# A finer table of TensorE's steps, other places of the steps beside it, and VectorE's weight subtraction cut in two in the last stage

## The chip, the cores and the metric

The program runs on one core of one Trainium2 chip. The metric is the device time of one execution in microseconds (us), as the median of three runs of the same program.

## What is computed

A sequence of 256 tokens of width 1024, in float32, goes through two layers of one kind and then through two of another, and at the end through a norm.

```python
for l in range(2):                                    # first block
    h = h + 0.5 * rms_norm(swiglu(rms_norm(h, g1), w_gate, w_up, w_down), p1)      # 1024 -> 2816 -> 1024
    u = rms_norm(h, mix_pre_g[l])
    (a_b, a_c, a_x, b_u, c_q, c_k, c_v, d_q, d_k, d_v, d_f, gate_logits) = split(u @ w_in[l])
    y_a = (a_b * conv3(a_c * a_x)) @ a_w_out
    y_b = silu(layer_norm(conv31(glu(b_u)) + bias)) @ b_w_out
    y_c = difference_attention(c_q, c_k, c_v) @ c_w_out          # two softmaxes, the second times lambda
    y_d = forgetting_attention(d_q, d_k, d_v, d_f) @ d_w_out
    h = h + rms_norm((sum of sigmoid(gate) * y over the four) @ w_o[l], p2)
    h = h + 0.5 * rms_norm(swiglu(rms_norm(h, g2), ...), p3)
for l in range(2):                                    # second block, "hybrid"
    z = rms_norm(h, norm_g[l]) @ w_in_2[l]
    qa, ka = axial_rope(rms_norm(aq)), axial_rope(rms_norm(ak))  # heads normed and rotated
    oa = attention(qa, ka, va) * silu(ag)
    ob = windowed_attention_with_sink(rope(bq), rope(bk), bv) * silu(bg)
    qc = rms_norm(cq) @ c_wuq ; kv = rms_norm(ckv) @ c_wukv      # the latent branch
    oc = attention([qc_nope, rope(qc_rope)], [kc_nope, rope(ckr)], vc) * silu(cg)
    h = h + concat(oa, ob, oc) @ w_out[l]
out = rms_norm(h, final_g)
```

## The kernel before

Every weight is read once from HBM, in chunks of 128 partitions by up to 2048 columns, in the order in which they are used (LOAD). SyncE issues the loads into `raw`, a ring of five slots; the load of chunk c waits until chunk c - 5 has been used up (semaphore `used`). Precision is kept by splitting each number into a high and a low part: ScalarE rounds a chunk to `whi` (L696), VectorE subtracts it from `raw` and leaves `wlo` in the same slot (L1046, semaphore `lo_v`), and TensorE makes three products for each pair of tiles (`mm3`, L1573 to L1575). Activations are split in the same way (`xhi`, `xlo`). "split n" below is the step that does ScalarE's or VectorE's half of this for the chunk that stands n places after the first of the stage.

The stages follow each other on one stream: twice (feed-forward, "mix", feed-forward), then twice "hybrid". Between two stages stands `boundary`: the result is normed and added to h in two halves of 128 tokens (t = 0, 1), the next norm is made, TensorE turns it (`turns`, L1671), ScalarE copies the turned tile to `xhi` (L715) and VectorE subtracts (`low`, L1065). TensorE meanwhile begins the next stage on t = 0 (`wide_entry`, L1641 to L1647).

Inside mix and hybrid the order of each engine is a list that is made once: `mix_steps` and `hybrid_steps` give every step a number, the place, and sort by it. Whole chunks of weights stand at regular places, and the small steps of the attentions, the convolution and the norms are put between them: `scores` (q times k), `max` and `exp`, `weigh` (VectorE, one over the sum), `turn` (TensorE transposes the probabilities, L1907 in mix, L2056 in hybrid), `copy`, `values` (times v, L1921, L2071, L2079) and `o_copy`, and then `flip` (transposes of q and k, or of the result). Each engine runs its list strictly in order, and each step first waits for the semaphores of its inputs. So a step whose input is late holds up all that stands behind it on its engine. In the hybrid stage TensorE's chunks could be entered by other steps at their middle, between the two halves of tokens; in the mix stage not at all. SyncE's list is the order of the loads alone; GpSimd's holds the powers for the norms (L659), in the order in which they are needed.

The names that matter: `l_norm` (L1477, L1478) norms the latent columns, after `l_square` on ScalarE (L975) and GpSimd's power; `l_turn` (L2014) is TensorE's transpose of them. `ropeg` (L1434) folds gains into the rotation tables for `a_rotate`. `o_split` (L1389) makes the low part of an attention's result, and `turn` 5 of the mix stage waits for it, since both use the same bank.

Of the kernel before, what the change touches and what calls it, by code (L numbers as in the profile page):

```python
# [14 lines left out]
ALU = mybir.AluOpType  # L15
# [6 lines left out]
P = 128  # L22
# [159 lines left out]
def mix_steps():  # L182
# [10 lines left out]
    for slot, (kind, n) in enumerate(chunks):  # L193
        pe.append((slot + 0.5, kind, n))
# [5 lines left out]
    at(pe, (19.02, 21.02, 23.02, 25.04, 27.02, 29.02, 31.02, 33.02), "turn")  # L200
# [22 lines left out]
             16.55, 17.55, 18.55, 19.55, 21.05, 22.05, 23.05, 23.55, 24.55, 25.55, 26.55, 28.057, 28.55, 30.55, 31.0601,  # L223
# [3 lines left out]
    at(dve, (25.5, 28.5, 31.5, 34.5, 37.5, 40.5, 43.5, 46.5), "out")  # L227
# [4 lines left out]
             19.06, 20.06, 21.0447, 22.06, 23.06, 24.06, 24.1, 25.1, 25.5275, 26.08, 28.14, 29.08, 30.12, 31.08, 32.12,  # L232
# [8 lines left out]
    at(dve, (18.02, 20.02, 22.02, 24.02, 26.02, 28.02, 30.02, 32.02), "weigh")  # L241
# [35 lines left out]
def hybrid_steps():  # L277
# [11 lines left out]
    at(pe, (3.52,), "l_turn")  # L289
    at(pe, (6.02, 6.2376, 6.54, 6.56, 9.02, 9.04, 10.52, 10.54), "flip")  # L290
    at(pe, (6.58, 7.54, 9.06, 9.54, 10.04, 10.58, 11.04, 12.04, 12.54, 14.04), "scores")
    at(pe, (7.52, 8.52, 9.5539, 10.02, 10.56, 11.02, 12.02, 12.52, 14.0607, 14.52), "turn")
    at(pe, (7.58, 8.54, 9.9373, 10.08, 10.62, 11.08, 12.08, 12.58, 14.08, 14.54), "values")
    at(act, (0.91, 1.9031, 1.91, 2.91, 4.6801, 5.91, 6.91, 8.91, 9.0669, 9.2882, 10.91, 11.3652, 12.91, 13.91, 14.4), "split", range(3, 18))
    at(act, (1.4, 1.9, 3.9, 4.0105, 4.0985, 4.2, 5.2, 5.7, 7.4, 7.9, 9.4, 9.9), "take", TAKES)
    at(act, (2.54,), "l_square")
    at(act, (3.52,), "l_hi")
    at(act, (6.02, 6.52, 6.54, 6.56, 9.02, 9.04, 10.52, 10.54), "flip_copy")
    at(act, (6.6, 7.56, 9.08, 9.56, 10.06, 10.6, 11.36, 12.06, 12.56, 14.06), "exp")
    at(act, (7.52, 8.52, 9.52, 10.02, 10.56, 11.32, 12.02, 12.52, 14.02, 14.52), "copy")  # L300
# [28 lines left out]
def program(nc, stream, x_in, pre_gain, post_gain, par1, par2, cst_in, out):  # L329
    ctx = ExitStack()  # L330
    with ctx:
# [704 lines left out]
        def _(dve):  # L1036
# [31 lines left out]
            def boundary(X, i, q, ch, share=None, last=False):  # L1068
# [6 lines left out]
                for t in range(NT):  # L1075
                    for n in range(2):
# [11 lines left out]
                        if t and not last:  # L1088
                            low(X + 1, 0, n)
# [1144 lines left out]
```

## Time and profile before

| | |
|---|---|
| median of 3 runs | 1691.02 us (1689.95 to 1692.52) |
| the profiled execution | 1691.12 us |
| its span, from the first to the last instruction | 1689.3 us |
| TensorE (PE) busy | 1646.0 us, 97% of the span |
| VectorE (DVE) busy | 1098.7 us, 65% |
| ScalarE (ACT) busy | 815.8 us, 48% |
| granted TensorE clock | 0.997 of full speed |
| read from HBM | 290.23 MB, 172 GB/s over the span |

The span is 1.8 us shorter than the execution's own time; the rest lies before the first and behind the last instruction. The first block fills the span up to about 1403 us, the two hybrid stages what is left. A row of the timeline gives the start, the duration, the engine, the source line and in brackets how long the engine was idle just before it and what ended the wait.

### The profile page before, as it was taken

The page shows a single profiled execution, that of the slowest core. Times are in us where ns is not written, and L with a number is a line of the kernel's source. Part 1 is how long each engine was busy: PE and PEld are TensorE (multiplying, and loading weights), DVE is VectorE, ACT ScalarE, POOL GpSimd, SP SyncE. Part 2 cuts the span into 40 slices and gives each one's busy share as a digit, 9 for nine tenths or more (in the row PEclk, how much of TensorE's full clock was granted, in tenths as well). Part 3 has the DMA queues.
Part 4 walks back from the last instruction along what each step waited for, and adds up shares of the span by engine and source line. Part 5 has one row for each costly group of instructions (what it writes and reads, how often), then busy time and mean ns, then how long its engine had stood idle before and what let it go on. Part 6 is the DMA issues. An engine that isn't in the chain of part 4 may idle for free.

```text
span 1689.3 us, 21552 instructions
## 1 busy us (share of the span) xinstructions
PE 1646.0 (97%) x8719; PEld 1395.1 (83%) x8719; DVE 1098.7 (65%) x1314; ACT 815.8 (48%) x1116; POOL 36.5 (2%) x60
## 2 busy tenths in 40 slices
PE   8999999999999999999999999999999998999997
PEld 7888799978887888788888998788888887778776
DVE  6444668898666454655456799975665455766665
ACT  5443544454445443454445454544544446664653
POOL 0000000000000000000000000000000000000000
PEclk9999999999999999999999999999999999999999
DMA  8555465444556555565546545355555545224421
GB/s 311 196 179 199 165 219 178 162 175 150 175 174 218 181 195 182 179 216 181 194 155 224 189 168 193 126 174 195 192 206 193 181 150 162 100 93 141 135 75 50
DMA packets 67427, 292.70 MB, mean 173 GB/s; under 512 B 7152, under 2 KB 11648, under 8 KB 51456
## 3 DMA queue, kind: packets, MB, share of 16 engines
q1 hardware_dynamic: 63984, 279.47, 48.2%
q10 hardware_dynamic: 3344, 11.85, 2.0%
q8 instruction: 69, 1.13, 0.3%
q14 instruction: 30, 0.25, 0.0%
HBM read 290.23 MB, written 1.06 MB: 172 GB/s over the span
## 4 chain that ended last, share of the span: by engine, by line
PE 82%; DVE 9%; issue 3%; ACT 3%; DVEq 2%; DMA 1%; POOL 0%; ACTq 0%; POOLq 0%; SPq 0%
PE ps L1573 24%; PE ps L1575 24%; PE ps L1574 24%; DVE wlo L1046 3%; PE ps L2045 2%; PE ps L1736 1%; DVE mix L1243 1%; DVEq L1248 1%; PE ps L2071 1%; PE ps L1671 1%; ACT tmp L699 1%; PE ps L2056 1%; PE ps L1708 1%; PE ps L1641 1%; DVE small L1335 1%
## 5 line engine op out<-in xcount | busy, mean ns | idle before, releaser
L1046 DVE TENSOR_TENSOR wlo<-raw,whi 128x2048 fp32r<-128x2048 f32 (+2 forms) x269 | 601.2, 2243 | 259.4 <-ACT whi L696 253.9
L696 ACT ACTIVATE whi<-raw 128x2048 fp32r<-128x2048 f32 (+2 forms) x269 | 500.3, 1872 | 130.7 <-DMA raw<-stream 129.4
L1573 PE MATMUL ps<-whi,xhi 128*128 128x512 f32 (+1 forms) x1024 | 404.1, 395 | 1.1 <-ACT mix L960 1.1
L1575 PE MATMUL ps<-whi,xlo 128*128 128x512 f32 (+1 forms) x1024 | 396.2, 387 | 0.0
L1574 PE MATMUL ps<-wlo,xhi 128*128 128x512 f32 (+1 forms) x1024 | 396.2, 387 | 0.0
L1573 PE MATMUL ps<-whi,yar 128*128 128x512 f32 x620 | 245.5, 396 | 2.0 <-DVE yar L1560 1.5
L1574 PE MATMUL ps<-wlo,yar 128*128 128x512 f32 x620 | 241.0, 389 | 0.0
L1575 PE MATMUL ps<-whi,yar 128*128 128x512 f32 x620 | 241.0, 389 | 0.0
L1573 PEld LDWEIGHTS ps<-whi,xhi 128*128 128x128 f32 x1024 | 192.8, 188 | 40.7 <-issue 4.5
L1575 PEld LDWEIGHTS ps<-whi,xlo 128*128 128x128 f32 x1024 | 192.7, 188 | 39.0
L1574 PEld LDWEIGHTS ps<-wlo,xhi 128*128 128x128 f32 x1024 | 192.9, 188 | 35.3
L1573 PE MATMUL ps<-xhi,whi 128*128 128x256 f32 (+1 forms) x720 | 207.5, 288 | 0.0
L1574 PE MATMUL ps<-xlo,whi 128*128 128x256 f32 (+1 forms) x720 | 203.6, 283 | 0.0
L1575 PE MATMUL ps<-xhi,wlo 128*128 128x256 f32 (+1 forms) x720 | 203.5, 283 | 0.0
L1573 PEld LDWEIGHTS ps<-whi,yar 128*128 128x128 f32 x620 | 116.4, 188 | 30.8 <-issue 7.2
L1573 PEld LDWEIGHTS ps<-xhi,whi 128*128 128x128 f32 (+1 forms) x720 | 136.3, 189 | 3.3 <-issue 0.9
L1574 PEld LDWEIGHTS ps<-xlo,whi 128*128 128x128 f32 (+1 forms) x720 | 136.4, 189 | 1.9
L1575 PEld LDWEIGHTS ps<-xhi,wlo 128*128 128x128 f32 (+1 forms) x720 | 136.3, 189 | 0.5
L1575 PEld LDWEIGHTS ps<-whi,yar 128*128 128x128 f32 x620 | 116.4, 188 | 24.3
L1574 PEld LDWEIGHTS ps<-wlo,yar 128*128 128x128 f32 x620 | 116.5, 188 | 23.0
L758 ACT ACTIVATE yar<-ps 128x512 fp32r<-128x512 f32 x44 | 26.3, 597 | 177.8 <-PE ps L1736 177.8
L1243 DVE SCALAR_TENSOR_TENSOR mix<-mix,par 128x256 f32<-128x256 f32 x240 | 105.2, 480 | 5.3
(217 smaller groups left out, 1361.6 us busy)
## 6 DMA issues: line engine op xcount, KB each, us to landing
raw<-stream SPq DMA_DIRECT2D x262, 512.0 KB, 4.7
raw<-stream SPq DMA_DIRECT2D x122, 1024.0 KB, 4.8
raw<-stream SPq DMA_DIRECT2D x22, 384.0 KB, 3.9
gpre<-pre_gain ACTq DMA_DIRECT2D x8, 512.0 KB, 4.2
gpost<-post_gain ACTq DMA_DIRECT2D x6, 512.0 KB, 5.3
mix<-cum ACTq DMA_DIRECT2D x2, 1024.0 KB, 6.8
raw<-stream SPq DMA_DIRECT2D x6, 256.0 KB, 6.8
raw<-stream SPq DMA_DIRECT2D x4, 320.0 KB, 4.4
```

Of the source, the lines that this page charges most:

```text
L696: A(whi[:, s, 0:w], raw[:, s, 0:w], ACT.Copy).then_inc(hi_ready, 1)
L699: A(tmp[:, n * 512:(n + 1) * 512], src, ACT.Square, scale=1.0 / 32, accum_out=rq[:, t, col + n:col + n + 1]).then_inc(sq_done, 1)
L758: A(hhi[hbuf(g)].rearrange("p m t -> p (m t)"), bank(2), ACT.Copy).then_inc(hhi_done, 1)
L1046: TT(wlo[:, s, 0:w], raw[:, s, 0:w], whi[:, s, 0:w].bitcast(F32), ALU.subtract).then_inc(lo_v, 1)
L1243: ins = STT(out=acc_b[:, m, :], in0=v, scalar=w, in1=acc_b[:, m, :], op0=ALU.mult, op1=ALU.add)
L1248: dve.drain()
L1335: dve.tensor_reduce(sm[:, 8:12], prob[:, :, 0:nk], AX, ALU.max)
L1573: pe.matmul(dst, lh, rh, start=first, stop=False)
L1574: pe.matmul(dst, lh, rl, start=False, stop=False)
L1575: return pe.matmul(dst, ll, rh, start=False, stop=last)
L1641: pe.matmul(dst, xhi[:, kk, rows_], wide_k(whi, c + j, k), start=(kk == 0), stop=False)
L2045: ins = pe.matmul(sc[:, e, :], a[:, t * P:(t + 1) * P], b, start=True, stop=True)
```

## The change

Five things change.

1. TensorE's list is cut finer. In the hybrid stage a chunk of weights is now eight parts (two halves of tokens, each in four) and an output chunk two; in the mix stage every chunk is two. Only the places between the parts are new: the same matmuls are made, in the same order inside a chunk.
2. The places of nearly all steps of the hybrid stage are new, on TensorE, ScalarE and VectorE; in the mix stage those of `turn` 4 on TensorE and of six steps on VectorE: two taps of the convolution move forward (18 and 19 of the second half of channels), split 26 moves behind `values` 4, `out` 2 behind `values` 6, and two `weigh` get other numbers without passing anything.
3. In the hybrid stage VectorE's split of a chunk is two steps, `half_split` (the first half of the columns) and `split` (the second half), each of half the width; the wait for `whi` is in the first, `lo_v` is raised by the second. In the new table the two stand next to each other for each of the 15 chunks.
4. In `boundary`, where a gain is applied (`share`), VectorE's last subtraction for t = 0 (`low(X + 1, 0, 1)`) moves from ahead of the update of h for t = 1 to behind it.
5. The wait for the rotation tables (`cst_in_s`) moves from `ropeg` to the start of VectorE's hybrid list, and `ropeg` moves behind `ck_rotate`.

SyncE's and GpSimd's lists are what they were, and no DMA changes its place among those of its queue.

```diff
@@ mix_steps (two of the lines of its table)
     for slot, (kind, n) in enumerate(chunks):
-        pe.append((slot + 0.5, kind, n))
+        for half in range(2):
+            pe.append((slot + 0.5 + half / 20, kind, (n, half)))
-    at(pe, (19.02, 21.02, 23.02, 25.04, 27.02, 29.02, 31.02, 33.02), "turn")
+    at(pe, (19.02, 21.02, 23.02, 25.04, 27.1998, 29.02, 31.02, 33.02), "turn")
@@ hybrid_steps (the parts, and one of the lines of its table)
     for p in range(AT_WOUT):
-        for half in range(2):
-            pe.append((p + half / 2 + 0.4, "chunk", p, half))
+        for part in range(8):
+            pe.append((p + (0.4, 0.425, 0.45, 0.475, 0.9, 0.925, 0.95, 0.975)[part], "chunk", p, part // 4, part % 4))
     for n in range(4):
-        pe.append((AT_WOUT + n / 2 + 0.4, "out", n))
+        for part in range(2):
+            pe.append((AT_WOUT + n / 2 + 0.4 + part / 20, "out", n, part))
+    at(dve, (1.9244, 1.9679, 2.4195, 4.1735, ...), "half_split", range(3, 18))
@@ VectorE
-            def split(ch):
+            def split(ch, half=None):
...
-                dve.wait_ge(hi_ready, ch + 1)
                 w = chunk_width(ch)
-                TT(wlo[:, s, 0:w], raw[:, s, 0:w], whi[:, s, 0:w].bitcast(F32), ALU.subtract).then_inc(lo_v, 1)
+                cut = slice(w // 2 if half == 1 else 0, w // 2 if half == 0 else w)
+                if half != 1:
+                    dve.wait_ge(hi_ready, ch + 1)
+                ins = TT(wlo[:, s, cut], raw[:, s, cut], whi[:, s, cut].bitcast(F32), ALU.subtract)
+                if half != 0:
+                    ins.then_inc(lo_v, 1)
@@ boundary
-                        if t and not last:
+                        if t and not last and not (share and n):
                             low(X + 1, 0, n)
                     dve.drain()
                     if share:
...
                                 op0=ALU.mult, op1=ALU.add).then_inc(h_ready, 1)
+                        if t:
+                            low(X + 1, 0, 1)
                         mean_square(q + (4 * t + 4), t, 2)
                         normed(t, i * 2 + (2 * t + 2))
@@ VectorE, hybrid
+                dve.wait_ge(cst_in_s, 32)
                 for step in HYB_DVE:
                     kind, n = step
-                    if kind == "split":
-                        split(ch + n)
+                    if kind == "half_split":
+                        split(ch + n, 0)
+                    elif kind == "split":
+                        split(ch + n, 1)
                     elif kind == "ropeg":
                         dve.wait_ge(par_in, l * 16 + (16 * DEPTH + 16))
-                        dve.wait_ge(cst_in_s, 32)
@@ TensorE: features, wide_tokens and rows_of take the parts (one of the three)
-            def wide_tokens(c, b, t):
+            def wide_tokens(c, b, t, ks=range(4)):
                 half = WIDE[c][2]
-                for k in range(4):
+                for k in ks:
...
+                if 3 not in ks:
+                    return
@@ TensorE, hybrid
-                        _, p, half = step
+                        _, p, half, part = step
...
                         if name in Z_PAIRS:
-                            if i == 0:
+                            if i == 0 and part == 0:
                                 hyb_free(pe, l, p, half)
-                            wide_tokens(c, half, half)
+                            wide_tokens(c, half, half, (part,))
```

What that does to the lists is seen at three places. In the rows an instruction reads: line, operation, out<-in, shape and what it waits for.

The first is TensorE's list in the mix stage, behind the chunk at place 26. `ps<-cst,prob` is `turn` 4, `ps<-mix` is `scores` 5, `ps<-whi,...` are matmuls with weights. Before:

```order
L1575 MATMUL ps<-whi,xlo 128x512
L1907 MATMUL ps<-cst,prob 128x128 [waits o_read,p_ready]
L1907 MATMUL ps<-cst,prob 128x128 x7
L1892 MATMUL ps<-mix 128x256 [waits nm_ready]
L1892 MATMUL ps<-mix 128x256 x3
L1573 MATMUL ps<-whi,xhi 128x512 [waits lo_v]
```

And with the change:

```order
L1586 MATMUL ps<-whi,xlo 128x512
L1911 MATMUL ps<-mix 128x256 [waits nm_ready]
L1911 MATMUL ps<-mix 128x256 x3
L1926 MATMUL ps<-cst,prob 128x128 [waits o_read,p_ready]
L1926 MATMUL ps<-cst,prob 128x128 x7
L1584 MATMUL ps<-whi,xhi 128x512 [waits lo_v]
```

`scores` 5 has passed `turn` 4; on VectorE, between `values` 3 and `scores` 5, a split of 2048 columns (split 26) has gone and stands behind `values` 4.

The second is ScalarE's list at the start of the hybrid stage. `mix<-ps` are the copies of the latent columns, `tmp,rq<-mix` is `l_square`, `yar<-ps` is the copy behind `l_turn`. Before:

```order
L967 ACTIVATE mix<-ps 128x352 [waits wide_done]
L967 ACTIVATE mix<-ps 128x352 [waits used]
L696 ACTIVATE whi<-raw 128x768 [waits landed3]
L696 ACTIVATE whi<-raw 128x512 [waits landed4]
L975 ACTIVATE tmp,rq<-mix 128x192 [waits evac_a]
L977 ACTIVATE tmp,rq<-mix 128x128
L975 ACTIVATE tmp,rq<-mix 128x192 [waits evac_a]
L977 ACTIVATE tmp,rq<-mix 128x128
L696 ACTIVATE whi<-raw 128x2048 [waits landed0]
L996 ACTIVATE yar<-ps 128x256 [waits lat_t]
```

And with the change:

```order
L699 ACTIVATE whi<-raw 128x768 [waits landed3]
L970 ACTIVATE mix<-ps 128x352 [waits wide_done]
L970 ACTIVATE mix<-ps 128x352 [waits used]
L978 ACTIVATE tmp,rq<-mix 128x192 [waits evac_a]
L980 ACTIVATE tmp,rq<-mix 128x128
L978 ACTIVATE tmp,rq<-mix 128x192 [waits evac_a]
L980 ACTIVATE tmp,rq<-mix 128x128
L699 ACTIVATE whi<-raw 128x512 [waits landed4]
L999 ACTIVATE yar<-ps 128x256 [waits lat_t]
```

`l_square` now stands ahead of the split of 512 columns and its wait for a load, and the split of 2048 columns behind the copy. On TensorE `l_turn` has moved one half chunk (12 matmuls) forward.

The third is TensorE's list in the hybrid stage around `turn` 1 (`ps<-cst,gpost`) and `values` 1 (`ps<-probT_b,mix`). Before:

```order
L1575 MATMUL ps<-whi,xlo 128x384
L2056 MATMUL ps<-cst,gpost 128x128 [waits pt_ready,p_ready]
L2056 MATMUL ps<-cst,gpost 128x128 x7
L2079 MATMUL ps<-probT_b,mix 128x128 [waits o_read,evac_a,pt_ready]
L2079 MATMUL ps<-probT_b,mix 128x128 x7
```

And with the change (three quarter chunks, of which the matmuls of two are left out here, and `values` 0 now stand between the two):

```order
L2077 MATMUL ps<-cst,gpost 128x128 [waits pt_ready,p_ready]
L2077 MATMUL ps<-cst,gpost 128x128 x7
L1584 MATMUL ps<-whi,xhi 128x384 [waits evac_a]
L1585 MATMUL ps<-wlo,xhi 128x384
L1586 MATMUL ps<-whi,xlo 128x384
L2100 MATMUL ps<-probT,mix 128x128 [waits evac_a,qkt_a,pt_ready]
L2100 MATMUL ps<-probT,mix 128x128 x7
...
L2100 MATMUL ps<-probT_b,mix 128x128 [waits o_read,evac_a,pt_ready]
L2100 MATMUL ps<-probT_b,mix 128x128 x7
```

What stood directly behind its supplier now has matmuls with weights in between.

## Rows read from the trace of the kernel before

**Rows 1.** The page: busy time by engine

```profile
PE 1646.0 (97%) x8719; PEld 1395.1 (83%) x8719; DVE 1098.7 (65%) x1314; ACT 815.8 (48%) x1116; POOL 36.5 (2%) x60
```

**Rows 2.** Waits of TensorE over the whole span: us in total, times, longest

```profile
PE ps L1671 <- DVE mix L1059: 6.1, 6, 2.4
...
PE ps L1907 <- DVE mix L1365: 4.6, 2, 2.3
PE ps L2056 <- DVE gpost L1543: 3.2, 6, 1.0
PE ps L2045 <- ACT mix L1004: 2.8, 4, 0.7
PE ps L2079 <- ACT probT_b L1025: 2.2, 2, 1.1
PE ps L2014 <- DVE mix L1478: 2.1, 2, 1.2
```

**Rows 3.** Five windows: length, busy PE, PEld, DVE, ACT, POOL; clock, DMA share, GB/s

```profile
1409.30:1530.00 120.70, 110.99 (x634) 92.54 (x633) 81.37 (x139) 72.35 (x151) 5.09 (x6) 1.00 0.32 109
1550.70:1672.00 121.30, 112.25 (x633) 93.69 (x633) 81.04 (x143) 69.45 (x148) 5.08 (x6) 0.99 0.30 103
1455.58:1460.01 4.43, 3.85 (x19) 3.08 (x19) 3.21 (x4) 3.28 (x8) 0.00 (x0) 1.00 0.40 168
1596.93:1602.25 5.32, 5.32 (x18) 4.33 (x18) 3.80 (x5) 3.87 (x8) 0.00 (x0) 0.68 0.36 149
1457.07:1459.43 2.36, 2.36 (x13) 2.04 (x12) 2.17 (x3) 1.21 (x6) 0.00 (x0) 1.00 0.13 49
```

**Rows 4.** Timeline of VectorE at the first boundary

```profile
201.07 0.69 DVE L1083 SCALAR_TENSOR_TENSOR thb<-ps,gpost 128x512 f32<-128x512 f32 x1
201.67 0.68 DVE L1065 TENSOR_TENSOR xlo<-ps,xhi 128x512 fp32r<-128x512 f32 x1
202.46 1.41 DVE L1095 SCALAR_TENSOR_TENSOR h<-thb,rs,h 128x512 f32<-128x512 f32 x2
```

**Rows 5.** Timeline of GpSimd there, then of TensorE

```profile
201.24 0.55 POOL L659 TENSOR_TENSOR rs<-rtmp,halft 128x1 f32<-128x1 f32 x1 [4.55 <-DVE rtmp L1051]
...
203.71 1.98 PE L1647 MATMUL ps<-whi,xlo 128*128 128x512 f32 x8
206.44 1.32 PE L1671 MATMUL ps<-cst,mix 128*128 128x128 f32 x8 [0.75 <-DVE mix L1059]
```

**Rows 6.** Timeline of TensorE in the first mix stage

```profile
366.75 1.07 PE L1907 MATMUL ps<-cst,prob 128*128 128x128 f32 x8 [2.29 <-DVE mix L1365]
367.74 1.14 PE L1892 MATMUL ps<-mix 64*128 64x256 f32 x8
...
382.38 1.03 PE L1907 MATMUL ps<-cst,prob 128*128 128x128 f32 x8
```

**Rows 7.** Timeline of VectorE there

```profile
368.60 2.29 DVE L1046 TENSOR_TENSOR wlo<-raw,whi 128x2048 fp32r<-128x2048 f32 x1
...
381.07 0.68 DVE L1389 TENSOR_TENSOR yar<-ps,yar 128x512 fp32r<-128x512 f32 x1
```

**Rows 8.** Timeline of ScalarE, then of VectorE, at the start of the first hybrid stage

```profile
1409.41 0.46 ACT L967 ACTIVATE mix<-ps 128x352 f32<-128x352 f32 x1 [2.95 <-PE ps L1647]
...
1412.56 0.63 ACT L696 ACTIVATE whi<-raw 128x512 fp32r<-128x512 f32 x1 [1.95 <-DMA raw<-stream]
1413.09 0.35 ACT L975 ACTIVATE tmp<-mix 128x192 f32<-128x192 f32 x1
...
1416.39 0.35 DVE L1478 SCALAR_TENSOR_TENSOR mix<-mix,rs,par 128x128 f32<-128x128 f32 x1
```

**Rows 9.** Groups of VectorE by shape: xcount | busy us, mean ns | idle before

```profile
L1046 DVE TENSOR_TENSOR wlo<-raw,whi 128x2048 fp32r<-128x2048 f32 x253 | 577.8, 2291 | 252.8 <-ACT whi L696 247.5
...
L1231 DVE TENSOR_TENSOR mix<-tmp,mix 128x1024 f32<-128x1024 f32 x12 | 14.7, 1226 | 0.9
```

**Rows 10.** DMA issues: KB each, median us from issue to landing

```profile
raw<-stream SPq DMA_DIRECT2D x122, 1024.0 KB, 4.8
```

More of the change, by code:

```diff
@@ L292, in hybrid_steps @@
[L292 to L298, printed above, removed]
@@ L306, in hybrid_steps @@
-    at(dve, (2.52,), "ropeg")
-    at(dve, (2.54,), "l_norm")
-    at(dve, (3.52,), "l_lo")
-    at(dve, (5.52,), "cq_rotate")
-    at(dve, (5.54,), "ck_rotate")
-    at(dve, (6.58, 7.54, 9.06, 9.54, 10.1064, 10.58, 11.04, 12.04, 12.54, 13.746), "max")
-    at(dve, (6.64, 7.62, 9.1, 9.62, 10.12, 10.66, 11.12, 12.1, 12.62, 14.1), "weigh")
-    at(dve, (8.02,), "a_mean")
-    at(dve, (8.02, 8.03), "a_rotate")
-    at(dve, (10.1, 10.11), "b_rotate")
-    at(dve, (10.9, 11.9, 12.9, 13.9), "gate")
-    at(dve, (11.1, 13.52, 15.02), "o_gate")
@@ L318, in hybrid_steps @@
-    at(dve, (11.7636, 13.53, 15.03), "o_low")
+        for part in range(2):
+            pe.append((AT_WOUT + n / 2 + 0.4 + part / 20, "out", n, part))
+    at(pe, (3.1197,), "l_turn")
+    at(pe, (5.4052, 6.1126, 6.4028, 6.4617, 8.9693, 9.1434, 10.4986, 10.6243), "flip")
+    at(pe, (6.9147, 7.4596, 9.4166, 9.906, 10.1901, 10.62, 10.9953, 11.4463, 11.9932, 12.9718), "scores")
+    at(pe, (8.4312, 8.5133, 9.9185, 10.3524, 10.9726, 11.0352, 12.4819, 12.935, 13.926, 14.0062), "turn")
+    at(pe, (8.9199, 8.966, 10.0387, 10.6179, 11.0096, 11.4335, 13.57, 13.9328, 14.016, 14.4175), "values")
@@ new lines, in hybrid_steps @@
+    at(act, (0, 0, 1.2009, 3.0722, 6.6004, 7.3136, 7.3484, 7.4213, 9.2391, 9.7951, 9.8875, 11.5645, 11.9264, 13.5379, 14.4885), "split", range(3, 18))
+    at(act, (0, 0, 4.8269, 5.2691, 5.8413, 6.4056, 6.4179, 6.4845, 7.4475, 7.5446, 9.2565, 9.5613), "take", TAKES)
+    at(act, (0.0543,), "l_square")
+    at(act, (1.5895,), "l_hi")
+    at(act, (6.4341, 6.5396, 6.7871, 7.1083, 8.5071, 8.847, 10.1345, 10.2488), "flip_copy")
+    at(act, (7.3987, 7.4945, 9.2075, 9.56, 9.721, 10.2087, 11.5264, 11.8831, 13.0461, 13.5386), "exp")
@@ new lines, in hybrid_steps @@
+    at(dve, (1.9245, 1.968, 2.4196, 4.1736, 5.8115, 6.8876, 6.8982, 9.0102, 10.2115, 10.2743, 11.024, 12.0727, 13.5213, 15.1284, 15.3818), "split", range(3, 18))
+    at(dve, (5.7505,), "ropeg")
+    at(dve, (2.2601,), "l_norm")
+    at(dve, (2.3134,), "l_lo")
+    at(dve, (5.57,), "cq_rotate")
+    at(dve, (5.69,), "ck_rotate")
+    at(dve, (6.88, 7.3612, 9.06, 9.54, 10.1035, 10.2663, 10.8198, 11.1546, 12.1934, 12.6207), "max")
+    at(dve, (8.0675, 8.0891, 9.3, 10.103, 10.2354, 10.2817, 11.9676, 12.5579, 12.6742, 13.0818), "weigh")
```

124 lines of the change are left out of this document (67 added, 57 removed).

## The prediction

> **What bounds the kernel now.** I read the page first: TensorE is busy for 1646.0 of 1689.3 us, and VectorE and ScalarE have a third and half of the span free [rows 1]. The amount of matmul work is the same before and after, so the time can only move by what TensorE waits, and all its waits together are the difference, 43 us. Next comes the list of TensorE's waits, which says for whom [rows 2]. Some 5 us lie at the start, where nothing is changed. Three places are left that the change touches: the turn of the second token half at the six boundaries, 6.1 us; one wait in each of the two mix stages for VectorE's L1365, 4.6 us; and a dozen kinds of short waits in the hybrid stages. The windows add those up [rows 3]: in the first stage 120.70 - 110.99 = 9.71 us idle, in the second 121.30 - 112.25 = 9.05. VectorE is busy for 81 of 121 us there and ScalarE for 72: neither is full, so these are waits for latency, where TensorE stands directly behind its supplier. The reader is to see in them that a wait of 0.6 to 1.2 us disappears as soon as that much other TensorE work is put in front of it.
>
> **The boundary.** VectorE reads thb until 201.07 + 0.69 = 201.76, then does the subtraction L1065 that is moved, and begins the update of h at 202.46 [rows 4]. The other thing that the update needs is GpSimd's power, done at 201.24 + 0.55 = 201.79 [rows 5]. Without the subtraction the update can begin at about 201.85, 0.6 us earlier, and squares, power, norm and turns follow it. TensorE waits there for 0.75 us [rows 5], so the gain fits inside. What is late next is the moved subtraction itself: behind the two updates (1.41 us) it ends at 201.85 + 1.41 + 0.6 = 203.9. The matmuls that read it are the second four of L1647's eight, from 203.71 + 1.98/2 = 204.7: 0.8 us of cover. It also sits in time that VectorE spent waiting for ScalarE's squares. At the sixth boundary (into the hybrid stage) the wait is 2.4 us [rows 2], the matmuls are narrower and those four may come late by 0.6, but in front of a longer wait. Six times 0.61: **3.7 us**. Bounds: nothing if the power is late, 6 x 0.7 = 4.2 at most.
>
> **The mix stage.** TensorE stands idle for 2.29 us until 366.75, because `turn` 4 waits for `values` 3 on VectorE, which goes from one instruction straight to the next there and is simply behind. With `scores` 5 first, 1.14 us of work fills the gap [rows 6]; its inputs are long there. The rest of the wait stays, since VectorE's sum of work up to there is the same (the two taps only trade places). What is late next is `turn` 5: it started at 382.38 [rows 6] and would now come at 381.2, but it waits for `o_split` 0, which ended at 381.07 + 0.68 = 381.75 [rows 7]. The 2.29 us split that is taken from 368.60 goes back in before it, so it ends no earlier (0.4 less where a short gap closes). So of 1.14 about 0.65 us stays, twice: **1.3 us**. Bounds 0.6 and 2.5. `out` 2 is put 3 us later, and its reader comes 10 us later; the same move frees `weigh` 7.
>
> **The hybrid stages.** I walked the new order step by step with the durations of the trace. At the start ScalarE copied the latent columns at 1409.41, then waited 1.95 us for a load, and came to the squares at 1413.09; now the squares follow the copy at 1409.8, 3.3 us earlier, so `l_norm` ends at 1413.4 and not at 1416.74 [rows 8]. TensorE arrives at `l_turn` at 1413.3, since it stands one half chunk (2.1 us) earlier: 0.2 us of its 1.2 are left. At `values` 1 (1.1 us) three quarter chunks, 3 x 0.59 from the half chunk of 2.36 [rows 3], and `values` 0 (2 us) stand in front: gone. Walked like this, the waits for L1543 (`weigh`), for the copies, for L1469 and for L1560 all fall under cover; VectorE has `weigh` done 1 to 9 us before TensorE asks. Two do not go. `scores` 2 still waits for the last `flip` copy, about 0.1. `scores` 3 waits for `exp` 2, which can only begin behind `scores` 2 and `max` and is over 4.43 - 1.56 = 2.9 us after `scores` 2 [rows 3], and the cover is four quarters as before: 0.58 stays. First stage: 9.71 - 0.88 = **8.8 us**.
>
> In the second stage the clock comes in. Between `scores` 2 and `scores` 3 the stretch takes 5.32 us where the first stage has 4.43, at a granted clock of 0.68 against 1.00 [rows 3]: for 3.4 us TensorE ran at 1.2 of its 2.4 GHz, after several waits in a row. Those waits are the ones that go. So 9.05 - 0.3 = **8.75**, and 5.32 - 4.43 = **0.9** if the clock holds; nothing of the latter if it falls anyway.
>
> **The cost of the halves.** The halves are neighbours, so nothing can use the point between them. A subtraction of 2048 columns takes 2291 ns, the like of 1024 columns 1226 [rows 9]: 161 ns more for a pair by durations, under 0.1 from start to start, 30 times 0.08 to 0.16 = 2.4 to 4.8 us of VectorE. I cost it at nothing: the cover is VectorE's 40 us of idle time in each stage. At four points (`l_turn`, `turn` 1, `scores` 2, `turn` 2) my walk leaves less than 0.3 us, and I take **1 us** off for these.
> The Trainium skill speaks against this step: "VectorE: DVE Perf Modes", section "The TRN2 errata — SBUF-src ops pay a fixed extra latency per instruction", says that one large tile pays the fixed cost once and many small ones each time, and gives an fp32 tensor_tensor (N + 151)/0.96 ns. By that formula, which the row of 2291 ns agrees with, a pair costs 157 ns more, 4.7 us in all.
>
> The `ropeg` step (1.3 us) moves behind `ck_rotate`; its reader comes some 15 us later. The wait for the tables was met hundreds of us before.
>
> **Sum.** 3.7 + 1.3 + 8.8 + 8.75 + 0.9 - 1 = 22.45, say 22.5 us. The profiled execution took 1691.12 us (span 1689.3), 0.1 above the median of the three runs: 1691.1 - 22.5 = **1668.6 us**, 1.3% faster.
>
> **Rivals.** (a) The walk is right, 0.52: between 1665.5 and 1671.5.
> (b) The waits come back at other places, 0.22. When TensorE is 9 us earlier at the end of a stage, every supplier must be so too, and VectorE and ScalarE have chains of their own (`scores`, `max`, `exp`, `weigh`, `copy`). Against it: they wait for TensorE much of the time. If half of the 17.5 us returns, 1668.6 + 8.8 = 1677.4.
> (c) The halves' cost reaches the path, 0.10: every 161 ns delays TensorE, 30 x 0.161 = 4.8 us: 1673.4. For it speaks that a split now often stands just before `max` or `weigh`; against it that most of those have over 1 us. The skill's rule named above, taken as deciding, would give this too: 1673.3.
> (d) More is gained than the waits show, 0.07: the busy time of pipelined matmuls may hide stalls, and the sixth boundary's low clock may go: 1660 to 1665.
> (e) Slower, 0.05: ScalarE now has splits 8, 9 and 10 ahead of `exp` 0 and `exp` 1, and waits for their loads in front of the softmax. Chunk 9's slot is free at about 1422, and `exp` 0 must be over at 1434.6, with 5 us of ScalarE work between: the load may take 7.5 us, and takes 4.8 [rows 10]. Only if loads there took over 18 us would each stage lose more than the whole change gains, and the time be 1695 or so.
> (f) The change doesn't do what it says, 0.04: the stages and boundaries are tied by chains through all engines, and the waits only change their names: a gain of 1 or 2 us, 1689.5.
>
> **Range and chances.** From the lower part of (a) and some of (d), over (c), to the far side of (b): 1664 to 1680, with 0.8 inside; (a)'s own is 1665.5 to 1671.5. A measurement of this kernel tells 0.2%, 3.4 us, from no change. Faster: (a) to (d), 0.91. Within: most of (f), 0.04. Slower: 0.05.
>
> **What would show it.** The wait of L1671's successor at five boundaries at 0.15 us, at the sixth 1.7; TensorE's wait before `turn` 4 at 1.15, with a new one of about 0.5 before `turn` 5; about 1 us idle in each hybrid stage, 0.58 of it before `scores` 3; no second fall of the clock; a pair of halves about 2.4 us long on VectorE. TensorE busy for 1646 us as before, less what the clock gave. I would be wrong if waits for `exp`, `weigh` or `whi` appear behind `scores` 4, where my walk has cover of several us, or if TensorE's busy time grew with the number of pieces.

## The result, and the profile after

The changed kernel takes 1662.92 us (median of 4 runs, 1661.71 to 1663.08), the kernel before beside it 1690.93: a ratio of 0.9832, 95% interval 0.9815 to 0.9849. It is 28.0 us faster, where 22.5 was forecast. The time lies just below the forecast range (1664 to 1680): the direction was right, the size too small. The profiled execution took 1662.86 us.

The page of the changed kernel, its span and its busy time by engine, against [rows 1]:

```profile
span 1661.1 us, 21582 instructions
...
PE 1637.4 (99%) x8719; PEld 1389.8 (84%) x8719; DVE 1099.6 (66%) x1344; ACT 815.8 (49%) x1116; POOL 36.9 (2%) x60
```

Span less busy time is what TensorE waits: 43.3 us before, 23.7 now, 19.6 less. But 19.6 is not the 28.2 us by which the span fell. TensorE's busy time fell too, by 8.6 us, from 1646.0 to 1637.4, with the same 8719 matmuls. That is the part which the forecast did not have.

Some of it is no gain. The first 13 us, up to the wait for L790 (now L793), hold the same instructions in both kernels, and the change doesn't touch them. TensorE alone there, before and after:

```profile
0.00:13.17 13.17, 7.66 (x37) 1.00 0.88 305
```

```profile
0.00:13.51 13.51, 6.29 (x38) 1.00 0.85 308
```

TensorE is busy for 1.4 us less and idle for 1.7 us more: the same matmuls were recorded shorter, and the waits took up the difference. In the 17 traces of this case that busy time lies between 6.1 and 7.7 us, and the idle time beside it makes up for it to within 0.6 us; why it varies is open (the clock reads 1.00 in both windows). So wherever busy times of two runs are compared below, these first 13 us are left out.

TensorE's waits in the changed kernel (line waited for by whom: us in total, times, longest), against [rows 2]:

```profile
PE ps L1926 <- DVE mix L1374: 2.4, 2, 1.2
PE ps L1721 <- ACT xhi L718: 1.6, 1, 1.6
...
PE ps L1926 <- DVE yar L1398: 1.3, 2, 0.7
PE ps L2066 <- ACT prob L1019: 1.2, 2, 0.6
PE ps L1684 <- DVE mix L1066: 1.0, 1, 1.0
...
PE ps L1584 <- DVE yar L1129: 0.6, 1, 0.6
PE ps L1660 <- DVE xlo L1072: 0.5, 1, 0.5
PE ps L2066 <- ACT mix L1007: 0.3, 2, 0.2
```

The 6.1 us at the boundaries have become 1.0 us at the sixth, 0.5 us in front of it (the moved subtraction is late there), and 0.12 to 0.14 us at the five others, too short for this list, which leaves single short waits out. Of the dozen kinds of waits in the hybrid stages, those of `scores` 3 (0.58) and `scores` 2 (0.15) are in the list, with `l_turn` and `turn` 1 (0.06 to 0.15) below it.

The two hybrid stages in windows of TensorE alone (us, busy time and matmuls; granted clock, DMA share, GB/s), from boundary turn to boundary turn and then to the end. The kernel before:

```profile
1402.50:1546.70 144.20, 134.20 (x752) 0.99 0.34 114
1546.70:1689.30 142.60, 127.32 (x704) 0.98 0.29 100
```

The changed kernel:

```profile
1398.20:1530.15 131.95, 130.67 (x752) 1.00 0.38 124
1530.15:1661.10 130.95, 123.72 (x704) 0.98 0.32 109
```

The stages are 12.25 and 11.65 us shorter, and busy time is 3.5 and 3.6 us of that, 7.1 in all; with the 1.4 us of the start that is nearly all of the 8.6. Up to the sixth boundary's turn the gain is 1402.5 - 1398.2 = 4.3 us. A part of the busy time is the clock. Two windows of the kernel before, and the first of them in the changed kernel:

```profile
1403.50:1406.90 3.40, 3.40 (x14) 0.50 0.47 145
1598.10:1601.40 3.30, 3.30 (x10) 0.50 0.21 84
```

```profile
1403.50:1406.90 3.40, 3.40 (x22) 1.00 0.72 198
```

TensorE had two stretches of 3.41 us at 1.2 instead of 2.4 GHz (low stretches from here on), one behind the 2.35 us wait at the sixth boundary, one in the second hybrid stage. Neither came again in this execution. `e2_oldhyb` below has the order of before in these stages and no such stretch in its profile; against it the stages of before are 1.4 and 1.4 us longer in busy time, and 1.7 and 0.85 in length (the second stretch shortened waits too). That is 2.8 of the 7.1 us. The other 4.3 are at full clock, and needed an explanation.

### The profile page after: what moved, and what is told of

Same layout as the page of the kernel before. It is cut to its first block, busy times and chain, and to the rows that moved or that the text cites. A ratio compares the mean times of both kernels' runs of the same rounds, so it can differ in the third digit from the quotient of the medians.

```text
span 1661.1 us, 21582 instructions
## 1 busy us (share of the span) xinstructions
PE 1637.4 (99%) x8719; PEld 1389.8 (84%) x8719; DVE 1099.6 (66%) x1344; ACT 815.8 (49%) x1116; POOL 36.9 (2%) x60
## 4 chain that ended last, share of the span: by engine, by line
PE 84%; DVE 7%; issue 2%; DVEq 2%; ACT 2%; DMA 1%; POOL 1%; ACTq 0%; POOLq 0%; SPq 0%
PE ps L1584 25%; PE ps L1586 24%; PE ps L1585 24%; DVE wlo L1051 3%; PE ps L2066 2%; PE ps L2092 1%; DVE mix L1252 1%; PE ps L1749 1%; DVEq L1257 1%; PE ps L2077 1%; PE ps L1684 1%; ACT tmp L702 1%; DMA raw<-stream 1%; DVE small L1344 1%; POOL rs L662 1%
## 5 line engine op out<-in xcount | busy, mean ns | idle before, releaser
L1051 DVE TENSOR_TENSOR wlo<-raw,whi 128x2048 fp32r<-128x2048 f32 (+4 forms) x299 | 602.6, 2033 | 259.9 <-ACT whi L699 254.6
```

Of the source, the lines that this page charges most:

```text
L1051: ins = TT(wlo[:, s, cut], raw[:, s, cut], whi[:, s, cut].bitcast(F32), ALU.subtract)
```

## Experiments

Two theories stood at the start. *Price*: a wait of TensorE costs more than its idle time, since the last matmul before it and the first behind it lose something too; what it costs beyond the idle time is called its price, and the place between the two matmuls a joint. *Order*: the hidden part comes from where the small steps (scores, turns, values) stand among the chunks, whatever waits.

**One part undone at a time.** Four kernels were made from the changed one. `e1_whole`: no halves in the hybrid stages.

```diff
-    at(dve, (1.9244, 1.9679, ...), "half_split", range(3, 18))
-                    if kind == "half_split":
-                        split(ch + n, 0)
-                    elif kind == "split":
-                        split(ch + n, 1)
+                    if kind == "split":
+                        split(ch + n)
```

> The changed kernel, but every subtraction of the hybrid stages is one whole instruction at the place of the first half. If the halves are hidden (my forecast), the time is that of the changed kernel, 1662.9 us, within 0.5 us, and VectorE is busy 3 to 5 us less. If their 161 ns a pair reach TensorE (rival c), up to 4.8 us less: 1658 to 1660 us.

Measured 1662.31 us (1661.59 to 1662.38), 0.6 less. Half of that lies in the first 13 us; the two hybrid stages are 0.3 us shorter together (131.76 + 130.82 against 131.95 + 130.95, windows below and above). VectorE is busy for 1097.9 us against 1099.6. So the halves cost VectorE 1.7 us (57 ns a pair, by busy time) and TensorE at most 0.3, where rival (c) had 4.8: it is out. Nor do they bring anything.

`e2_oldhyb`: the whole body of `hybrid_steps` is that of the kernel before (the chunks in eight pieces at its places, so that the pieces touch), with whole subtractions.

```diff
-            pe.append((p + (0.4, 0.425, ...)[part], "chunk", p, part // 4, part % 4))
+            pe.append((p + part // 4 / 2 + 0.4, "chunk", p, part // 4, part % 4))
-    at(pe, (3.1197,), "l_turn")
+    at(pe, (3.52,), "l_turn")
...
```

> The changed kernel with the hybrid stages' order of the kernel before on all three engines (whole subtractions too); boundary and mix stage stay changed. By the forecast's terms (idle time 8.8 + 8.75, clock 0.9, less 1) it is 17.5 us slower than the changed kernel: 1680.4. By the comparison of the traces (the two stages were 12.2 and 11.65 us shorter) it is 23.9 us slower, 1686.8; 1.6 us less, 1685.2, if the low clock behind the sixth boundary was caused by the wait there and so stays away. In both cases I expect a low clock of about 3.4 us again in the second stage, and TensorE's busy time per stage 2 us or more above the changed kernel's beside the clock.

Measured 1684.40 us (1683.46 to 1684.58): 22.1 us above `e1_whole`, which differs from it in nothing but that order, and between the two totals expected. The two pages, first `e1_whole`:

```profile
span 1660.6 us, 21552 instructions
...
PE 1638.2 (99%) x8719; PEld 1390.7 (84%) x8719; DVE 1097.9 (66%) x1314; ACT 815.6 (49%) x1116; POOL 36.6 (2%) x60
```

and `e2_oldhyb`:

```profile
span 1681.7 us, 21552 instructions
...
PE 1641.9 (98%) x8719; PEld 1391.0 (83%) x8719; DVE 1098.0 (65%) x1314; ACT 815.2 (48%) x1116; POOL 36.5 (2%) x60
```

By the pages the idle time is 22.4 against 39.8 us, 17.4 more, and the busy time 3.7 more. The two hybrid stages alone, without the start, `e1_whole` and then `e2_oldhyb`:

```profile
1398.02:1529.78 131.76, 130.61 (x753) 1.00 0.37 124
1529.78:1660.60 130.82, 123.68 (x704) 0.99 0.32 109
```

```profile
1397.46:1539.95 142.49, 132.78 (x752) 1.00 0.34 115
1539.95:1681.70 141.75, 125.91 (x704) 0.99 0.29 101
```

Idle time is 17.3 us more, close to what the forecast took out of the hybrid stages (8.8 + 8.75), and busy time 4.4 us more. Here the clock has no part in it: in both profiles the only low stretch begins behind TensorE's last matmul. So the hidden part is real, and belongs to the hybrid order: 2.2 us a stage, with 12 waits fewer in each, 0.18 us a wait. The low clock that was expected in the second stage did not come in the profiled execution. That was the fastest of the five; the four others took 0.5 to 1.1 us longer at a mean clock of 0.998 against 0.999, which leaves room for one low stretch each.

`e3_oldbound`: the subtraction is back ahead of the update at all six boundaries.

```diff
-                        if t and not last and not (share and n):
+                        if t and not last:
                             low(X + 1, 0, n)
...
-                        if t:
-                            low(X + 1, 0, 1)
```

> The changed kernel with the subtraction back ahead of the update of h at all six boundaries. Idle time: 5 x 0.62 + 0.9 = 4.0 us back, 1666.9. If the 2.35 us wait at the sixth boundary is what made the clock fall behind it, the low clock of 3.4 us comes back there too and the time is 1668.5; if the clock fell because of the old hybrid order or of the two together, it stays away. If each wait had a price beyond its idle time even where it only gets shorter, 6 x 0.2 more: 1668.1 without the clock.

Measured 1666.79 us (1665.24 to 1667.25), 3.9 more. The list of waits has L1682 at 6.1 us, 6 times, again, and the low clock behind the sixth boundary came back in the profiled execution (first of the two fences below). There it costs some 1.4 us, and the first 13 us and an ffn stage happen to be 0.7 us shorter than in the changed kernel, so that 3.9 is close to the 4.0 of idle time in part by luck. The run of 1665.24 us had a mean granted clock of 1.000 and so had no such stretch: the wait makes it possible, not certain.

`e4_oldmix`: the mix stage's places of the kernel before.

```diff
-    at(pe, (19.02, 21.02, 23.02, 25.04, 27.1998, ...), "turn")
+    at(pe, (19.02, 21.02, 23.02, 25.04, 27.02, ...), "turn")
...
```

> The changed kernel with the mix stage's places of the kernel before. By the idle time in the traces 0.5 + 0.4 = 0.94 us slower, 1663.9; by my forecast's term 1.3, 1664.2. Neither is told from no change by the total alone; the windows of the two mix stages should show the wait of 2.3 us before turn 4 again and none before turn 5.

Measured 1664.68 us (1664.20 to 1665.76), 1.8 more. The profiled execution, the slowest of the four, had a low clock at the wait of 2.3 us in both mix stages, where the kernel before had none in its profile; the two account for more than the excess over 0.94. Windows of `e3_oldbound`, then of `e4_oldmix`:

```profile
1402.90:1406.20 3.30, 3.30 (x13) 0.50 0.44 161
```

```profile
366.50:369.80 3.30, 3.30 (x15) 0.50 0.42 179
1059.40:1062.70 3.30, 3.30 (x13) 0.50 0.10 42
```

**A wait by itself.** GpSimd has nothing to do in the ffn stages, and TensorE hardly waits there. So GpSimd is made to answer TensorE: it waits for the end of a matmul and writes a scratch tile, and TensorE waits for that. 8 groups in each of 4 ffn stages make 32 waits; nothing else is changed. `p1_ffn`:

```diff
+            def ping(c):
+                pool.wait_ge(used, c)
+                pool.memset(scr[:, :], 0.0).then_inc(pong, 1)
...
                     pe.wait_ge(h2_ready, f * NG + g)
+                    pe.wait_ge(pong, f * (NG - 3) + g)
                     rows(c, hhi[hbuf(g - 1)], hlo[hbuf(g - 1)], g == 1)
```

> The changed kernel with 32 waits more on TensorE, all in the four ffn stages (8 each), where it has next to none: ahead of the down matmuls of 8 groups TensorE waits until GpSimd, which has nothing else to do there, has seen the end of the matmul before and written 8 columns of a scratch tile. Theory 'price': each wait costs its idle time and about 0.2 us more, in the last matmul before it and the first after it, so TensorE's busy time rises by some 6 us over the 1637.4 of the changed kernel, and the total by that plus the idle time shown. Theory 'order' (the hidden part of the gain came from where small steps stand among the chunks): busy time the same within 1 us, and the total rises by the idle time alone.

Measured 1680.86 us (1680.58 to 1681.08), 17.9 more. `p2_ffn_long`, with the longer answer:

```diff
-                pool.memset(scr[:, :], 0.0).then_inc(pong, 1)
+                pool.tensor_tensor(scr[:, 0:1], epst[:, 0:1], halft[:, 0:1], ALU.pow).then_inc(pong, 1)
```

> The same 32 waits, but GpSimd answers with a power of one column (about 550 ns) in place of a write of 8 columns (about 100 ns), so each wait is some 0.45 us longer. 'Price': the busy time rises by the same amount as with the short waits (a fixed price for each), while the idle time rises by 32 x 0.45 = 14 us more. If the price grows with a wait's length, the busy time rises about twice as much or more. 'Order': no rise in either. A low clock, if it comes, is told apart by the granted clock.

Measured 1701.87 us (1695.21 to 1705.11, with mean clocks from 0.996 to 0.999; the clock accounts for at most half of that spread, the rest is open). Its profiled execution took 1699.50 us. From the two traces, page and list of waits, first `p1_ffn`:

```profile
PE 1646.7 (98%) x8719; PEld 1388.1 (83%) x8719; DVE 1099.7 (65%) x1344; ACT 815.3 (49%) x1116; POOL 40.1 (2%) x92
...
PE ps L1596 <- POOL scr L678: 9.4, 30, 0.3
```

then `p2_ffn_long`:

```profile
PE 1647.8 (97%) x8719; PEld 1389.4 (82%) x8719; DVE 1099.8 (65%) x1344; ACT 815.3 (48%) x1116; POOL 57.5 (3%) x92
...
PE ps L1596 <- POOL scr L678: 28.1, 32, 2.5
```

Busy time rose by 1646.7 - 1637.4 = 9.3 us with waits of 0.31 us, and by 10.4 with waits of 0.88 on average (29 of 0.78, three of 1.27 to 2.47). Without the first 13 us that is 8.7 and 9.7, and one low stretch of the second, some 1.4 us by the two above, leaves 8.3. Waits of nearly three times the length, the same extra: **a fixed price of 0.26 to 0.27 us a wait, beyond its idle time.** No small step moved here, so *order* can't give this. (How a wait divides into idle time and price hangs on the recorded ends of the matmuls, which the profile models. The whole does not: from the start of the matmul before a wait to the start of the 25th behind it, `p1_ffn` takes 0.59 us longer than the changed kernel at the same place.)

`h1_hyb` places 9 such waits in each hybrid stage, ahead of chunks 4 to 8 and 10 to 13:

```diff
                         if half == 0 and part == 0:
                             ready(c)
+                            if p in PINGS:
+                                pe.wait_ge(pong, l * len(PINGS) + PINGS.index(p) + 1)
```

> The changed kernel with 9 such short waits in each hybrid stage, ahead of chunks 4 to 8 and 10 to 13 (GpSimd writes 8 columns when the chunk before has been done); order of the steps unchanged. 'Price': TensorE's busy time rises by about 0.2 us for each wait that shows, 3 to 4 us for 18, as it did with the hybrid stage's order of before (4.5 us of busy time for some 25 waits more). 'Order': no rise of the busy time.

Measured 1667.20 us (1667.01 to 1667.45), 4.3 more. Only 10 of the 18 show, at 0.27 to 0.31 us; at the others a small step stands between and the answer has come. Busy time is 1639.3 us; without the first 13 us it is 2.1 more: 0.2 a wait.

`q1_halfchunk` asks what the finer cut is worth: small steps stand behind whole half chunks only.

```diff
-            pe.append((p + (0.4, 0.425, 0.45, 0.475, 0.9, 0.925, 0.95, 0.975)[part], ...))
+            pe.append((p + (0.4, 0.4, 0.4, 0.4, 0.9, 0.9, 0.9, 0.9)[part], ...))
```

> The changed kernel, but a small step of the hybrid stages can stand only behind a whole half chunk, as before, and not between quarters: 18 steps move behind the half that they stood in, all else keeps its place. 'Price': busy time changes by 0.2 us times the number of waits that come or go. 'Order': the small steps now stand next to each other more often (turn 0 and 1, values 0 and 1, flips 4 and 5 in a row), and busy time changes with the same waits. In the sum of idle time I expect 1 to 3 us more in each stage, since cover between the steps is lost: 1665 to 1669 us.

Measured 1674.14 us (1673.55 to 1674.24), 11.2 more: half of what the hybrid stages gained, and far more than I expected. There are 10 waits more, most of them between steps that now touch; in its list of waits:

```profile
PE ps L2066 <- ACT prob L1019: 2.7, 4, 0.8
...
PE ps L2077 <- ACT probT L1028: 2.4, 2, 1.2
PE ps L2100 <- ACT mix L990: 2.1, 2, 1.1
PE ps L2092 <- ACT probT L1028: 1.8, 2, 0.9
PE ps L2066 <- ACT gpost L1019: 1.7, 2, 0.8
```

Busy time is 1639.5 us; without the first 13 us it is 1.8 more, again some 0.2 for each wait more.

**What sets the price.** It was 0.27 at one joint and about 0.2 in the hybrid stages. Two more kernels put the 32 waits at other joints of the ffn stages. `p4_before_turn`: ahead of the four transposes of the hidden layer, with the answer triggered by the matmul there.

```diff
                         if half == 0:
+                            if g < NG - 2:
+                                pe.wait_ge(pong, f * (NG - 3) + g)
                             turn_hidden(g - 1)
```

> The changed kernel with 32 waits in the ffn stages again, at another joint: between a 512-column matmul and the four transposes of the hidden layer (GpSimd writes 8 columns when the matmul is done). Without a wait the matmul before runs 161 ns on while the first transpose has begun, so if the price beyond idle time is this overlap and a slower start, the busy time rises by about 32 x 0.2 = 6 to 8 us. If the price were the same everywhere, 32 x 0.29 = 9 us as with the first 32 waits.

Measured 1674.75 us (1674.63 to 1674.84). `p5_after_turn`: the same two lines behind `turn_hidden(g - 1)`, and GpSimd waits for the transposes.

> The same 32 waits between the last of the four transposes and the 512-column matmul behind it. Without a wait the transpose there runs 244 ns on while the matmul has begun, more than at the two other joints (161 and 162 ns). If the price is the overlap that the joint loses, the busy time rises by 32 x (0.244 + 0.08) = 10 us, more than the 9.3 of the first 32 waits; if it has to do with the width of the matmul before the wait (512 columns there, 128 here), it is smaller than there, 4 us or less.

Measured 1676.62 us (1676.53 to 1677.21). The waits are 0.22 us in both, and busy time without the first 13 us is 5.5 and 7.6 us more: 0.17 and 0.24 a wait. The order of the two is that of the overlaps, and not that of the widths. One joint in the three traces (start, us, instruction, idle before). `p1_ffn`:

```profile
35.64 0.39 PE L1598 MATMUL ps<-whi,xlo 128*128 128x512 f32 x1
36.34 0.47 PE L1596 MATMUL ps<-whi,yar 128*128 128x512 f32 x1 [0.31 <-POOL scr L678]
36.65 0.40 PE L1597 MATMUL ps<-wlo,yar 128*128 128x512 f32 x1
```

`p4_before_turn`:

```profile
29.87 0.39 PE L1598 MATMUL ps<-whi,xlo 128*128 128x512 f32 x1
30.48 0.66 PE L1761 MATMUL ps<-cst,tmp 128*128 128x128 f32 x4 [0.22 <-POOL scr L678]
```

`p5_after_turn`:

```profile
29.92 0.60 PE L1761 MATMUL ps<-cst,tmp 128*128 128x128 f32 x4
30.74 0.50 PE L1596 MATMUL ps<-whi,xhi 128*128 128x512 f32 x1 [0.22 <-POOL scr L678]
```

In a run without waits one 512-column matmul starts 0.227 us after another and is recorded for 0.389: it ends 0.162 us after the next has begun, and so did matmuls of 128 and 256 columns. With a wait for the end of the matmul before, the next can't begin before that end, so these 0.16 us come on top of the idle time. The first matmul behind it is slower as well: in `p1_ffn` its successor starts 0.31 us after it, not 0.23. Together 0.24; the starts of the next dozen matmuls slip by 0.04 more against the changed kernel, which makes 0.28 for 0.27 by busy time. At the transposes the overlap is 0.161 and the slower start costs 0.06 (0.66 us for four, 0.60 without the wait); the next dozen matmuls win 0.03 back, which leaves 0.19 for 0.17. Behind the transposes the overlap is 0.244, and the start is slow there with or without a wait: 0.24 to 0.26 for 0.24. So the price is the overlap that the joint loses, plus what the restart costs where it was not slow already.

**A version that beats both.** What is left in the list is in two places mere order. `v1_mix`, from `e1_whole`:

```diff
-    at(dve, (18.02, 20.02, 22.02, 24.02, 26.02, ...), "weigh")
+    at(dve, (18.02, 20.02, 22.02, 24.02, 25.53, ...), "weigh")
-    at(dve, (20.04, 21.0539, 24.04, 26.04, ...), "values")
+    at(dve, (20.04, 21.0539, 24.04, 25.54, ...), "values")
-    at(dve, (28.08, 30.08, 32.08, 36.04), "o_split")
+    at(dve, (28.05, 30.08, 32.08, 36.04), "o_split")
```

> The kernel with whole subtractions (1662.3 us) and three places changed in VectorE's mix table: the reciprocal of group 4 and its values step ahead of split 25 (whose chunk TensorE reads 9 us later), and the first o_split ahead of splits 26 and 27. TensorE's waits before turn 4 (1.21 us) and turn 5 (0.66 us) should both go, in each of the two mix stages. If a wait is worth its idle time, 3.7 us less: 1658.6. If each wait that goes wholly gives 0.3 us more, as the 32 inserted ones cost, 4.9 us less: 1657.4, with TensorE busy for 1.2 us less.

Measured 1658.71 us (1658.54 to 1659.44), 3.6 less than `e1_whole`: the idle time of the two waits and, it seems, no price. But a new wait came. `turn` 4, flip 0 and `turn` 5 in `e1_whole`, then in `v1_mix`:

```profile
366.13 1.06 PE L1923 MATMUL ps<-cst,prob 128*128 128x128 f32 x8 [1.21 <-DVE mix L1373]
...
374.23 0.61 PE L1949 MATMUL ps<-cst,mix 128*128 128x128 f32 x4
...
380.98 1.06 PE L1923 MATMUL ps<-cst,prob 128*128 128x128 f32 x8 [0.68 <-DVE yar L1397]
```

```profile
364.76 1.09 PE L1923 MATMUL ps<-cst,prob 128*128 128x128 f32 x8
...
373.23 0.66 PE L1949 MATMUL ps<-cst,mix 128*128 128x128 f32 x4 [0.17 <-DVE mix L1389]
...
379.20 1.04 PE L1923 MATMUL ps<-cst,prob 128*128 128x128 f32 x8
```

From `turn` 4 to flip 0 it is 8.47 us and not 8.10, 0.37 more for a wait of 0.17; from flip 0 to `turn` 5 it is 5.97 and not 6.75, 0.78 less for a wait of 0.68. So a price did come back at `turn` 5, 0.1 us, and the new wait took 0.2. At `turn` 4 the matmuls before it (64 rows) overlap the transposes by 0.07 us only, and it comes 1.37 us earlier, 0.09 of them from the start of the kernel, for a wait of 1.21. My 0.3 was the price of another joint.

`v2_scores0` (also `scores` 0 of the mix stage to 17.52 on TensorE and 16.045 on VectorE):

> The same, and scores 0 of the mix stage moves behind the first half of chunk 16 on TensorE (behind three taps on VectorE), so that its wait of 0.69 us for ScalarE's copy should go, twice. By idle time 1.4 us less than the run before, with 0.3 a wait 2.0 less: 1655.4 to 1657.2. What speaks against it: turn 0 may come to wait, since scores 0 is done 2.2 us later and my reading leaves it 0.3 us.

Measured 1657.99 us (1657.57 to 1658.38), 0.7 less, where 1.4 to 2.0 was expected. Both waits of 0.69 are gone, and the turn at the sixth boundary starts 1.66 us earlier than in `v1_mix`; the profiled execution then had a low stretch of 3.41 us, which `v1_mix` had not, and lost 1.2 us in it.

`v3_all` (also `l_turn` 3.1197 to 3.41, flip 5 9.1434 to 8.97, `scores` 3 9.906 to 9.93, `turn` 1 8.5133 to 8.91, `turn` 2 9.9185 to 9.9305):

> The same, and in the hybrid table l_turn one quarter later, flip 5 ahead of the last quarter of chunk 8, turn 1, scores 3 and turn 2 one quarter later. The waits of 0.13, 0.14, 0.05 and 0.56 us should go, twice: 1.8 us less by idle time; 8 waits at 0.2 us more, 3.4 less. 1652 to 1655.5.

Measured 1655.92 us (1655.69 to 1657.84), 2.1 less and just above the range expected, with one new wait of 0.51 us a stage (flip 5 for a copy of `values` 1). `v4_two` mends that and moves tap 24 of the convolution from 27.06 to 27.13:

> The run with all moved places (1655.9 us) and two corrections from its trace: flip 5 back behind the last quarter of chunk 8 (next to flip 4 it waited 0.51 us for a copy of values 1), and tap 24 of the mix stage behind the two o_scale steps on VectorE (flip 0 waited 0.17 us for them). Idle time: 2 x (0.51 - 0.15 + 0.17) = 1.1 us less, with the price of waits up to 1.7: 1654.2 to 1654.9.

Measured 1654.50 us (1654.03 to 1656.35): ratio to the kernel before 0.9788, interval 0.9773 to 0.9802, and 8.4 us below the changed kernel. The profiled execution was the slowest of its four (1656.35), with a low stretch at the same place as that of `v2_scores0`.

**The boundary's edit alone**, `b1_bound`, on the kernel before:

> The kernel before with the boundary's edit alone. By idle time 5 x 0.62 + 0.9 = 4.0 us faster than before, 1686.8; the waits there get shorter and do not go, so the price of 0.3 for a wait is not given back. If the wait of 2.35 us at the sixth boundary set off the low clock behind it, that is gone too: 1685.2. The low clock in the second hybrid stage should be there still, since that stage is as before.

Measured 1687.37 us (1685.46 to 1688.10) against 1692.38 of the runs beside it: ratio 0.9967, interval 0.9956 to 0.9978, 5.0 us faster. A part of that is the clock, 0.996 to 0.998 on average against 0.995 to 0.997 of the runs beside it; between the two profiles it is 3.0 us. The waits are as expected (0.12 at five boundaries). The low clock behind the sixth boundary is gone, the one in the second hybrid stage is there, and two have come in the mix stages, at waits of 2.28 us that had been there without one before.

## Why the prediction was too careful, step by step

**The step that failed** is the second sentence of its first part: "The amount of matmul work is the same before and after, so the time can only move by what TensorE waits". The work is the same, its busy time is not. The 28.2 us between the profiles are made up like this, beside the terms of the sum:

| | forecast | in the profiles |
|---|---|---|
| idle time at the boundaries and in the mix stages | 3.7 + 1.3 | 4.9 |
| idle time in the hybrid stages (`e2_oldhyb`), less what the halves take | 8.8 + 8.75 - 1 | 17.3 - 0.3 |
| clock, low stretch of the second hybrid stage | 0.9 | 0.85 |
| clock, low stretch behind the sixth boundary | 0 | 1.7 |
| price of the waits that went wholly | 0 | 4.4 |
| start and ffn stages, which the change doesn't touch | 0 | some -0.6 |

So the terms that failed are the two that the sum put at nothing: the price of 24 waits, 4.4 us, and the first low stretch, 1.7 us. This is what rival (d) said, at 0.07: the experiments give it, and rule out (b), (c), (e) and (f).

**The boundary**, 3.7 forecast: 4.0 us of idle time by the lists. Five turns wait 0.12 to 0.14 us (forecast 0.15); no price came back, since these waits only got shorter. At the sixth the wait is 1.0 + 0.48 where 1.7 was forecast; the 0.48 is a new wait and costs 0.64 us (the starts of before and `b1_bound` around it). What the sum left out is the clock behind it. VectorE at the first boundary, against [rows 4]:

```profile
201.38 0.68 DVE L1090 SCALAR_TENSOR_TENSOR thb<-ps,gpost 128x512 f32<-128x512 f32 x1
202.14 1.42 DVE L1102 SCALAR_TENSOR_TENSOR h<-thb,rs,h 128x512 f32<-128x512 f32 x2
203.47 0.69 DVE L1072 TENSOR_TENSOR xlo<-ps,xhi 128x512 fp32r<-128x512 f32 x1
```

**The mix stage**, 1.3 forecast: 0.94 of idle time. `turn` 4 waits for 1.21 us (1.15), and in front of `turn` 5 stand 0.66 and 0.68, not 0.5, against [rows 6]:

```profile
364.09 1.13 PE L1911 MATMUL ps<-mix 64*128 64x256 f32 x8
366.44 1.06 PE L1926 MATMUL ps<-cst,prob 128*128 128x128 f32 x8 [1.21 <-DVE mix L1374]
...
381.29 1.06 PE L1926 MATMUL ps<-cst,prob 128*128 128x128 f32 x8 [0.66 <-DVE yar L1398]
```

**The hybrid stages.** The walk's idle time, 17.55, was right (17.3 by `e2_oldhyb`), with `scores` 3 at 0.58 as forecast. The 1 us taken off for four thin points was not needed in full: `l_turn`, `turn` 1 and `scores` 2 wait 0.06 to 0.15. What the sum lacked is 4.4 us of busy time. It could have been estimated from the profile of before: a matmul recorded for 0.389 us every 0.227 says that 0.16 us hang over each, and 24 waits gone at 0.16 are 3.8 us. At some joints the real price is below that (64 rows to 128: 0.07) and at others above (0.27).

**The clock**: 0.9 forecast, 2.6 in the profiles (1.7 + 0.85). In the profile of `e2_oldhyb`, with every wait of the hybrid stages back, no low stretch came; in that of `e4_oldmix` two did, at waits that had none before. Which wait is followed by one changes from run to run: the 36 runs of the kernel before that stand beside the experiments lie between 1689.3 us (mean clock 0.998) and 1694.4 (0.995), with medians of 1690.6 to 1692.4 by batch, the four of the changed kernel within 1.4 us, at 0.999. I estimate from these clocks and times that the gain from the clock is some 2 to 5 us on average; only a bound could be forecast.

**The halves**, nothing forecast, nothing measured. A half of 1024 columns takes 1219 ns on average; the Trainium skill, "VectorE: DVE Perf Modes", section "The TRN2 errata — SBUF-src ops pay a fixed extra latency per instruction", gives (N + 151)/0.96 ns, 1224, and the trace agrees. The pair costs less than the 157 ns that follow from it, 57 ns of busy time, since the two overlap. The rule spoke against the step, and its sign is right, but at most 0.3 us of it reaches the path.

**The range.** Its lower end came from (a) and "some of (d)". With the bound above (3.8 us) and one low stretch more, (a)'s own range would have begun at 1660.

## What to carry to other kernels

TensorE starts its next matmul before the last has ended, and loses that overlap at a wait: price a wait of TensorE at its idle time and the overlap (0.16 us here; the measured prices go from 0.07 to 0.27 by the joint), a fixed sum that comes back only when the wait goes wholly. So many short waits are worth more than the list of waits says, and shortening one is worth only its idle time. Cutting the big work into quarters, so that a small step always finds cover of the size of the copy it waits for, gave half of the hybrid stages' gain, by `q1_halfchunk`, which keeps the order that was made for quarters (the best order for half chunks was not looked for, and might lose less); the halves of the subtraction gave nothing: nothing was put between them. And check where the busy time of two runs differs before reading it: here 1.4 us of it lay in the first 13 us, where nothing had changed.

## What the runs showed of the hardware that I had not expected

- A wait of 0.3 or of 0.9 us costs the same 0.26 to 0.27 us of extra busy time between 512-column matmuls, and a wait of 0.22 us 0.17 ahead of transposes, 0.24 behind them.
- Low stretches of TensorE's clock (1.2 GHz, 3.41 us each, 0.85 to 1.7 us lost) began 0.4 to 1.6 us behind waits of 2.3 to 2.5 us, in `v2_scores0` and `v4_two` 0.7 and 0.9 us behind waits of 0.5 and 1.0 us with 0.9 us of matmuls between them, and in the second hybrid stage of before behind several waits in a row, the last of 0.58 and 0.69 us; but the same waits pass without one in other runs. No trace here says which, so 1 or 2 us between two orders may be this alone.
